# A hybrid encoder layer with PEER experts: U's products in three rounded passes, the dense stage unrolled, and half a tile's expert rows fetched during routing

## The chip, the cores and the metric

One core of a Trainium2 chip runs one launch of the program. The metric is the device time of the launch in microseconds (us); lower is better. Everything is float32 in and out.

## The reference

Attention, projections and norms come first; the part that the change touches is the PEER layer. For each of 1152 tokens (1024 prompt, 128 sample) it takes the 16 best of 128 x 128 experts for each of 8 heads, so 128 experts a token:

```python
def blk(tb):                                   # tb: 128 tokens x 1024
    q = (tb @ wq).reshape(128, 8, 2, 128)
    sc = einsum('thpd,pnd->thpn', q, subkeys)
    sv, si = top_k(sc, 16)
    cand = sv[:, :, 0, :, None] + sv[:, :, 1, None, :]
    cv, ci = top_k(cand.reshape(128, 8, 256), 16)
    e = i1 * 128 + i2                          # i1, i2: si at ci // 16, ci % 16
    g = softmax(cv)
    h = einsum('thkd,td->thk', u[e], tb)
    return einsum('thk,thkd->td', gelu(h) * g, v[e])
```

u and v are 16384 x 1024 each. The result is added to the residual, and a last RMS norm follows.

## The kernel before

The program runs stages one after the other: lead, sample attention, projection (with the fetched rows of the sample tile), window attention, `decide` and `dense`. The change touches the last two.

**decide** (the routing stage) goes over the eight prompt tiles of 128 tokens, i = 1 to 8. In iteration i, TensorE does the stick-breaking attention of tile i (i pairs of blocks, `attend`), then the output projections, the queries of tile i-1 (`queries`, 16 slices w), their scores, and the merge with `w_o`. VectorE meanwhile ranks the scores of tile i-2: `halves_best`, `pairs_best`, `experts_of`, `weigh`; between them it forms the residual (`residual`) and norm of its neighbours. It has about the same order as TensorE, with semaphores in both directions.

A tile is then treated in one of three ways. A *dense* tile (i = 1 to 4) is computed against all experts in `dense`; for it a matrix G of gates (expert x token) must be in memory. For the *sent* tiles (1 to 3) GpSimd scatters the weights into G, one indirect DMA for each of 128 columns, 384 in all (`scatter_head`, L1512). For the *hot* tile (4) TensorE builds G out of one-hot matrices that VectorE makes (`one_hots`), in 32 chunks of four tokens; `WOVEN` says how many chunks go into each attention pair. A *fetched* tile (5 to 8) stores its normed activations, indices and weights.

**dense** has 128 blocks of 128 experts. In block b TensorE does `hidden(b)`, eight float32 products of U's block with the 512 dense tokens, and `values`, eight products for a group of GB = 4 earlier blocks, into four banks. ScalarE applies gelu, VectorE multiplies with G (`gate`) and adds the value banks to qacc (`take`). Beside it run the fetched tiles, 4 rows a block and 512 in all: GpSimd gathers row r of u and v for 128 tokens (`gathers`, 1 MB) into a ring of SL = 8 slots, VectorE multiplies and sums (`products`, two rows), ScalarE takes their gelu, and VectorE adds the weighted v row to acc one pair later (`add_rows`), which frees the slot. The code is in loops whose body covers eight blocks, with waits against registers; the very first body stands outside.

SP issues the loads in one fixed order (L2020 U, L2023 V, L2013 on). U's block b goes into one of GB = 4 buffers and waits for the product of b-4. V has two groups of buffers; the first V load of group n (`v_rows`, j = 0) waits until the values of group n-2 are done, and all later loads stand behind that wait:

```python
sp.dma_start(gb[u][:], o["G"][bass.ts(n, GB)].rearrange("b p t -> p b t")).then_inc(g_in[u], 16)
for j in range(GB):
    u_rows(GB * n + j, j)
    if j == 0 and not (number(n) and n < 2):
        sp.wait_ge(v_done, 2 * DENSE * (n - 1))
        sp.sem_inc(sp_past, 1)
    v_rows(GB * n + j, u, j)
```

## Time and profile before

| | us |
|---|---|
| median of 3 runs | 4029.32 (4026.34 to 4032.59) |
| profiled execution | 4026.89 |
| its span | 4025.2 |
| mean granted clock of TensorE | 0.935 of full speed |

| share of the span | PE | VectorE | ScalarE | GpSimd |
|---|---|---|---|---|
| busy | 88% | 65% | 21% | 41% |

Each engine's busy time comes from its own instructions; loads of TensorE's weights overlap its products. The granted clock is the share of 2.4 GHz that TensorE was given. A float32 product of 512 columns appears as two records, so eight products are 16 records (x16). `decide` runs from about 1100 to 2148 us, `dense` from there to the end. The rows further down are all from this one execution.

### The profile page before, as it was taken

How to read it: one execution, taken by the hardware profiler on the slowest of the kernel's cores; microseconds unless marked ns; L12 is line 12 of the kernel's file. 1: busy time of each engine (PE TensorE's matmuls, PEld its weight loads, DVE VectorE, ACT ScalarE, POOL GpSimd, SP SyncE). 2: the span in 40 equal slices, each digit the busy share in tenths (PEclk: the TensorE clock that was granted, in tenths of full speed). 3: DMA queues.
4: the chain of work that ended last, by engine and by line, in shares of the span. 5: the costliest groups of instructions: out<-in, count | busy, mean ns of one | idle time of the engine just before them, and what ended most of it. 6: DMA issues, size and time to landing. Idle time of an engine off the chain costs nothing. (4 is left out here: it accounts for less than half of the span.)

```text
span 4025.2 us, 44686 instructions
## 1 busy us (share of the span) xinstructions
PE 3549.7 (88%) x14147; PEld 2107.2 (52%) x14147; DVE 2617.7 (65%) x5036; ACT 841.0 (21%) x1599; POOL 1631.8 (41%) x1245
## 2 busy tenths in 40 slices
PE   8997878776699999988862899999999999999998
PEld 6445567776457667656651344444444444444443
DVE  0451878883405435344464988888888878888886
ACT  1451211112423444354510000010001000010001
POOL 0000077770000777777773433334333334333331
PEclk9899889887799999999986999999999999999999
DMA  7793399995765656666856999999999999999994
GB/s 256 315 408 146 105 383 407 384 391 210 254 222 185 151 128 160 143 138 116 169 123 250 391 406 388 388 400 405 400 416 403 397 372 400 388 398 388 382 387 186
DMA packets 424246, 1201.21 MB, mean 298 GB/s; under 512 B 150473, under 2 KB 215417, under 8 KB 345337
## 3 DMA queue, kind: packets, MB, share of 16 engines
q0 software_dynamic: 168496, 680.80, 45.8%
q1 hardware_dynamic: 187600, 505.84, 34.2%
q10 hardware_dynamic: 67968, 12.45, 1.9%
q8 instruction: 78, 1.28, 0.1%
q14 instruction: 104, 0.84, 0.1%
HBM read 1127.33 MB, written 72.68 MB: 298 GB/s over the span
## 5 line engine op out<-in xcount | busy, mean ns | idle before, releaser
L2066 POOL DMA_INDIRECT d_ring<-peer_uv,d_idx x512 | 655.4, 1280 | 1087.6 <-DVEq L2120 981.9
L2223 PE MATMUL d_ps<-d_xd,d_u 128*128 128x512 f32 x2048 | 908.5, 597 | 99.9 <-DMA d_u<-u_blocks 81.1
L2234 PE MATMUL d_ps<-d_v,d_a 128*128 128x512 f32 x2048 | 914.1, 600 | 43.3 <-DVE d_a L2126 36.5
L1512 POOL DMA_INDIRECT G<-c_cellg,c_cell x384 | 617.5, 1608 | 436.6 <-DVE c_cellg L1641 233.5
L2118 DVE SCALAR_TENSOR_TENSOR d_acc<-d_ring,d_aw,d_acc 128x1024 f32<-128x1024 f32 x512 | 657.7, 1285 | 102.1 <-DVE d_acc L2118 66.9
L2223 PEld LDWEIGHTS d_ps<-d_xd,d_u 128*128 128x128 f32 x2048 | 391.8, 192 | 596.0 <-issue 584.3
L2234 PEld LDWEIGHTS d_ps<-d_v,d_a 128*128 128x128 f32 x2048 | 393.3, 193 | 545.5 <-issue 544.8
L2106 DVE SCALAR_TENSOR_TENSOR d_ring<-d_ring,d_xn 128x1024 f32<-128x1024 f32 x512 | 605.9, 1221 | 97.3 <-DMA d_qacc<-ys 51.5
L840 POOL DMA_INDIRECT a_x<-peer_uv,a_rowu x128 | 154.2, 1205 | 547.8 <-DVE a_rowv L910 505.3
L2188 ACT ACTIVATE d_ge<-d_h (+1 forms) x256 | 52.0, 203 | 1204.9 <-DVE d_ring L2106 1204.6
L1037 PE MATMUL a_ps<-a_w_low,a_x_high 128*128 128x256 f32 (+1 forms) x704 | 204.3, 290 | 61.7 <-DVE a_w_low L852 45.8
L1917 PEld LDWEIGHTS c_ps<-c_mT,c_chunk 128*128 128x128 f32 x2048 | 232.3, 194 | 4.9 <-issue 3.4
L1917 PE MATMUL c_ps<-c_mT,c_chunk 128*128 128x128 f32 x2048 | 232.6, 277 | 1.1 <-ACT c_mT L1754 1.1
L1037 PE MATMUL a_ps<-a_w_high,a_x_low 128*128 128x256 f32 (+1 forms) x704 | 202.8, 288 | 0.0
L1037 PE MATMUL a_ps<-a_w_high,a_x_high 128*128 128x256 f32 (+1 forms) x704 | 202.6, 288 | 0.0
L2133 DVE TENSOR_TENSOR d_qacc<-d_ps,d_qacc 128x512 f32<-128x512 f32 x256 | 167.8, 684 | 42.6 <-PE d_ps L2234 42.5
L937 DVE SCALAR_TENSOR_TENSOR k_acc<-a_x,a_gw,k_acc 128x1024 f32<-128x1024 f32 x128 | 164.5, 1285 | 33.4 <-DVE k_acc L937 25.2
L840 POOL DMA_INDIRECT a_x<-peer_uv,a_rowv x128 | 165.5, 1293 | 43.5 <-issue 36.6
L932 DVE SCALAR_TENSOR_TENSOR a_x<-a_x,k_xg 128x1024 f32<-128x1024 f32 x128 | 153.8, 1225 | 35.0 <-DMA a_x<-peer_uv,a_rowu 32.4
L1037 PEld LDWEIGHTS a_ps<-a_w_low,a_x_high 128*128 128x128 f32 x704 | 139.6, 198 | 63.5 <-DVE a_w_low L852 47.4
L1828 PE MATMUL c_ps<-c_q,c_k 64*128 64x128 f32 (+1 forms) x1152 | 158.4, 289 | 14.3 <-DVE c_mask_b L1533 14.2
L1828 PEld LDWEIGHTS c_ps<-c_q,c_k 64*128 64x128 f32 (+1 forms) x1152 | 142.4, 198 | 49.1 <-issue 30.2
(360 smaller groups left out, 4134.4 us busy)
## 6 DMA issues: line engine op xcount, KB each, us to landing
c_chunk<-wq SPq DMA_DIRECT2D x128, 512.0 KB, 5.0
d_u<-u_blocks SPq DMA_DIRECT2D x128, 512.0 KB, 18.7
d_v<-v_blocks SPq DMA_DIRECT2D x128, 512.0 KB, 16.5
s_kc<-sb_kT SPq DMA_DIRECT2D x32, 1024.0 KB, 9.5
s_vc<-sb_v SPq DMA_DIRECT2D x32, 1024.0 KB, 7.4
c_chunk<-w_m SPq DMA_DIRECT2D x64, 512.0 KB, 5.5
d_gb<-G SPq DMA_DIRECT2D x32, 1024.0 KB, 34.5
G<-b_zeros SPq DMA_DIRECT2D x32, 768.0 KB, 8.3
```

The source lines that it names most:

```text
L840: pool.indirect_dma_start(out=ring[:, k % RB], out_offset=None, in_=rows, in_offset=bass.IndirectOffsetOnAxis(ap=source[:, k % P:k % P + 1 ...
L937: nc.vector.scalar_tensor_tensor(acc[:], ring[:, r], aw[:, s:s + 1], acc[:], ALU.mult, ALU.add).then_inc(summed, 1)
L1037: last = nc.tensor.matmul(out, lhsT(left, k), rhs(right, k), start=(k == 0 and n == 0), stop=(k == KC - 1 and n == 2))
L1512: pool.indirect_dma_start(out=grid, out_offset=bass.IndirectOffsetOnAxis(ap=cell[q][:, s:s + 1], axis=0), in_=cell_g[q][:, s:s + 1], in_of ...
L1828: last = nc.tensor.matmul(ps[:, bank + par, c * P:(c + 1) * P], k_sb[p % 2][0:rows, x], q_sb[0:rows, x], start=(c == 0 or n > 0 and stop), ...
L1917: last = nc.tensor.matmul(ps[:, QUERY[w // 4], (w % 4) * P:(w % 4 + 1) * P], wq[:, c * P:(c + 1) * P], xT[:, c], start=(c == 0), stop=(c = ...
L2066: pool.indirect_dma_start(out=ring[:, b], out_offset=None, in_=a["peer_uv"], in_offset=bass.IndirectOffsetOnAxis(ap=idx8[par][:, b:b + 1], ...
L2106: last = nc.vector.scalar_tensor_tensor(ring[:, b, 0:D], ring[:, b, 0:D], 1.0, xn[T % 2][:], ALU.mult, ALU.mult, accum_out=h[:, bass.ds(co ...
L2118: nc.vector.scalar_tensor_tensor(acc[T % 2][:], ring[:, b, D:], aw[:, bass.ds(col + n, 1)], acc[T % 2][:], ALU.mult, ALU.add).then_inc(sum ...
L2133: nc.vector.tensor_tensor(part, ps[:, VB + c % 4, :], part, ALU.add).then_inc(v_taken, 1)
L2223: last = nc.tensor.matmul(ps[:, HB + x % 2, :], ub[j][:, k], xd[:, k].rearrange("p t q -> p (t q)"), start=(k == 0), stop=(k == KC - 1))
L2234: last = nc.tensor.matmul(ps[:, VB + c % 4, :], A[u][j][:, q * P:(q + 1) * P], vb[u][j][:, half * 512:half * 512 + 512], start=(j == 0), s ...
```

## The change

In **dense**, U's block and the dense activations are each split in a high part, which is the value rounded to the narrower format of TensorE's fast float32 mode (`F32R`), and a low part, the rest. `hidden` then does three products, low x high, high x low and high x high, in place of one: 24 a block. ScalarE copies the high part of U (`high`), VectorE subtracts to get the low part (`low`), one block ahead. U's buffers go from four to two, which `low` frees, the ring of rows from eight slots to six. All loops are unrolled and wait on constants; the index copies on GpSimd go. The order of SP's first loads changes; qacc is loaded last.

The **tiles** are shifted: tile 1 is now fetched, tiles 2 to 5 are dense, of which 2 and 3 are sent (256 scatters) and 4 and 5 are hot (64 chunks). Of tile 1's 128 rows, EARLY = 64 are handled in decide: GpSimd gathers the 64 u rows and then the 64 v rows there (4 KB for each token) into a ring of eight, and VectorE takes them at places given by `FETCH`, `LOOKUPS` and `AFTER`. `dense` has 448 rows left, 3.5 a block. Of the 64 chunks, 22 are woven into attention, and 14 each go beside the queries of tiles 6, 7 and 8 (`AMONG`), in banks 6 and 7.

The core of the diff (lines left out where there is "..."):

```diff
-DENSE, HOT = 4, 1
+DENSE, HOT = 4, 2
 FIRST_HOT = DENSE - HOT
 FETCHED = NT - 1 - DENSE
+EARLY = 64
...
-    WOVEN = [[0] * i for i in range(NT - 2)] + [[0] + [2] * 6, [0] + [3] * 6 + [2]]
+    WOVEN = [[0] * i for i in range(NT - 2)] + [[0, 2, 2, 2, 2, 1, 1], [0, 2, 2, 2, 2, 2, 1, 1]]
+    AMONG = 14
+    RB = 8
+    FETCH = [[0] * i for i in range(4)] + [[3, 3, 4, 4], [3, 3, 4, 4, 4], [2, 3, 3, 3, 3, 2], [2] * 7, [1] * 8]
+    LOOKUPS = [0, 0, 0, 0, 6, 6, 6, 0, 0]
+    AFTER = [0, 0, 0, 14, 6, 0, 2, 6, 4]
+    GELU_AT = 5
...
-    dense = lambda i: 1 <= i <= DENSE
-    hot_tile = lambda i: FIRST_HOT < i <= DENSE
-    sent = lambda i: 1 <= i <= FIRST_HOT
-    fetched = lambda i: i > DENSE
+    dense = lambda i: 2 <= i <= DENSE + 1
+    hot_tile = lambda i: 2 + FIRST_HOT <= i <= DENSE + 1
+    sent = lambda i: 2 <= i < 2 + FIRST_HOT
+    fetched = lambda i: i == 1 or i > DENSE + 1
+    rank = lambda i: 0 if i == 1 else i - DENSE - 1
+    among = lambda j: AMONG if j >= NT - 3 else 0
...
+                def gather(n):
+                    for k in range(issued[0], min(issued[0] + n, 2 * EARLY)):
+                        at = k % EARLY
+                        source = row_u if k < EARLY else row_v
+                        if k >= RB:
+                            pool.wait_ge(freed, k - RB + 1)
+                        pool.indirect_dma_start(out=ring[:, k % RB], out_offset=None, in_=rows,
+                                                in_offset=bass.IndirectOffsetOnAxis(ap=source[:, at:at + 1], axis=0)).then_inc(filled[k % RB], 16)
+                    issued[0] += n
...
+                pool.wait_ge(rows_ready, 3)
+                gather(RB + AFTER[3] + sum(FETCH[4]) + LOOKUPS[4] + AFTER[4])
+                for n in range(44):
+                    scatter(2)
+                    gather(1)
+                while sends[0] < P * FIRST_HOT:
+                    scatter(min(5, P * FIRST_HOT - sends[0]))
+                    gather(1)
+                gather(2 * EARLY - issued[0])
+                pool.wait_ge(scattered, 16 * P * FIRST_HOT)
...
                     for n, (table, test) in enumerate(((rise, ALU.is_ge), (pos[:, :, 1, 1:17], ALU.is_equal))):
+                        beside(3 * n)
                         step(nc.vector.tensor_tensor(hot, place[:, n, :, :, None].to_broadcast([P, 8, 16, 16]),
                                                      digit[:, n, None, None, :].to_broadcast([P, 8, 16, 16]), test), f"hot{n + 1}", j)
+                        beside(3 * n + 1)
...
+                def fetch(n):
+                    for k in range(fetches[0], fetches[0] + n):
+                        r, s = k % RB, k % EARLY
+                        if k == EARLY:
+                            dve.wait_ge(act_e, 1)
+                            nc.vector.tensor_tensor(aw[:, 0:EARLY], h_sb[:, 0:EARLY], gw_first[:, 0:EARLY], ALU.mult).then_inc(dve_e, 1)
+                            dve.wait_ge(dve_e, 1)
+                        dve.wait_ge(filled[r], 16 * (k // RB + 1))
+                        if k < EARLY:
+                            nc.vector.scalar_tensor_tensor(ring[:, r], ring[:, r], 1.0, xg[:], ALU.mult, ALU.mult,
+                                                           accum_out=h_sb[:, s:s + 1]).then_inc(freed, 1)
+                        else:
+                            if s:
+                                dve.wait_ge(summed, s)
+                            nc.vector.scalar_tensor_tensor(acc[:], ring[:, r], aw[:, s:s + 1], acc[:], ALU.mult, ALU.add).then_inc(summed, 1)
+                            dve.wait_ge(summed, s + 1)
+                            dve.sem_inc(freed, 1)
+                    fetches[0] += n
...
                         one_hots(WOVEN[i][n])
+                        fetch(FETCH[i][n])
...
-                    experts_of(i - 2)
+                    mixed = among(i - 1)
+                    one_hots(min(2, mixed))
+                    experts_of(i - 2, lambda n: (one_hots(mixed * (n + 1) // 7 - mixed * n // 7), fetch(LOOKUPS[i] // 6)))
+                    one_hots(mixed - min(2, mixed) - mixed * 6 // 7)
                     weigh(i - 2)
+                    fetch(AFTER[i])
...
-                halves_best(NT - 2)
+                halves_best(NT - 2, lambda n: one_hots((3, 3, 3, 3, 2)[n]))
+                fetch(2 * EARLY - fetches[0])
...
+                        for w in range(4 * g, 4 * g + 4):
+                            take(1 if w >= 16 - among(j) else 0, BESIDE)
...
+                    if i == GELU_AT:
+                        act.wait_ge(freed, EARLY)
+                        nc.scalar.activation(h_sb[:, 0:EARLY], h_sb[:, 0:EARLY], ACT.Gelu).then_inc(act_e, 1)
...
+                        if w == 16 - among(j) and j < NT - 1:
+                            pe.wait_ge(dve_m.sem, dve_m.at(j + 1, "gated_b"))
+                        spread_out(1 if w >= 16 - among(j) else 0, BESIDE)
...
-    SL = 8
-    TB = P // FETCHED
+    SL = 6
+    NU, NS = 2, 2
...
+    TILES = [0] + list(range(DENSE + 1, NT - 1))
+    STARTS = [0] + [P - EARLY + P * k for k in range(FETCHED)]
+    ROWS = STARTS[-1]
+    PAIRS = ROWS // 2
+    pairs_in = lambda b: range(PAIRS * b // P, PAIRS * (b + 1) // P)
...
+                def u_rows(b):
+                    if b >= NU:
+                        sp.wait_ge(u_split, b - NU + 1)
+                    sp.dma_start(ub[b % NU][:], a["u_blocks"][b]).then_inc(u_in[b % NU], 16)
+                def v_rows(b):
+                    n, u, j = b // GB, b // GB % 2, b % GB
+                    if n >= 2 and j == 0:
+                        sp.wait_ge(v_done, VC * (n - 1))
                     sp.dma_start(vb[u][j][:], a["v_blocks"][b]).then_inc(v_in[u], 16)
...
+                for n in range(2):
+                    sp.dma_start(xd[:, 4 * n:4 * n + 4], o["xd"][:, 4 * n:4 * n + 4].rearrange("p k t q -> p k (t q)")).then_inc(xd_in[n], 16)
+                    u_rows(n)
+                gates(0)
+                v_rows(0)
                 for dst, src in ((gw[:], o["gw"].rearrange("t p s -> p t s")), (gf[:], bass.AP(a["gf"].tensor, 0, [[0, P], [1, D]]))):
                     sp.dma_start(dst, src).then_inc(tabs, 16)
...
-                sp.dma_start(qacc[:], o["ys"][0:DENSE].rearrange("t p d -> p t d")).then_inc(qacc_in, 16)
...
+                for j in range(1, GB):
+                    if j > 1:
+                        u_rows(j)
+                    v_rows(j)
+                sp.dma_start(qacc[:], o["ys"][1:1 + DENSE].rearrange("t p d -> p t d")).then_inc(qacc_in, 16)
+                for n in range(1, NG):
+                    for j in range(GB):
+                        u_rows(GB * n + j)
+                        if j == 0:
+                            gates(n)
+                        v_rows(GB * n + j)
...
+                def low(b):
+                    dve.wait_ge(u_high_done, b + 1)
+                    nc.vector.tensor_tensor(u_low[b % NS][:], ub[b % NU][:], u_high[b % NS][:].bitcast(F32), ALU.subtract).then_inc(u_split, 1)
...
+                for b in range(P):
+                    if b:
+                        gate(b - 1)
+                    if b + 1 < P:
+                        low(b + 1)
+                    for c in (2 * (b - 1) % VC, 2 * (b - 1) % VC + 1):
+                        n = b // GB - 1 - (b % GB == 0)
+                        if n == 0 and c == 0:
+                            dve.wait_ge(qacc_in, 16)
+                        if n >= 0:
+                            take(n, c)
+                    for p in pairs_in(b):
+                        products(p)
+                        if p:
+                            add_rows(p - 1)
...
+                def high(b):
+                    act.wait_ge(u_in[b % NU], 16 * (b // NU + 1))
+                    if b >= NS:
+                        act.wait_ge(h_done, b - NS + 1)
+                    nc.scalar.activation(u_high[b % NS][:], ub[b % NU][:], ACT.Copy).then_inc(u_high_done, 1)
...
-                def hidden(b, x, j, round):
-                    pe.wait_ge(u_in[j], 16 * (round + 1))
-                    if not (number(b) and b < 2):
+                def hidden(b):
+                    pe.wait_ge(u_split, b + 1)
+                    if b >= 2:
                         pe.wait_ge(h_gelu, b - 1)
+                    x_parts, u_parts = (x_high, x_low), (u_high[b % NS], u_low[b % NS])
                     for k in range(KC):
-                        last = nc.tensor.matmul(ps[:, HB + x % 2, :], ub[j][:, k], xd[:, k].rearrange("p t q -> p (t q)"), start=(k == 0), stop=(k == KC - 1))
+                        if b == 0:
+                            pe.wait_ge(x_split, k + 1)
+                        for n, (left, right) in enumerate(((0, 1), (1, 0), (0, 0))):
+                            last = nc.tensor.matmul(ps[:, HB + b % 2, :], u_parts[left][:, k], x_parts[right][:, k],
+                                                    start=(k == 0 and n == 0), stop=(k == KC - 1 and n == 2))
                     last.then_inc(h_done, 1)
```

## Rows read from the trace of the kernel before

**Rows 1.** Windows: stretch, length; PE, PEld, DVE, ACT, POOL busy; clock, DMA share, GB/s

```profile
1174.00:2148.00 974.00, 836.60 (x5027) 620.18 (x5024) 463.98 (x1948) 373.22 (x565) 617.52 (x384) 0.93 0.63 145
...
2240.00:3985.00 1745.00, 1710.01 (x3952) 754.07 (x3952) 1481.65 (x2119) 147.60 (x400) 658.68 (x562) 0.99 0.98 390
...
2590.00:3100.00 510.00, 510.00 (x1189) 225.63 (x1188) 442.14 (x634) 48.46 (x124) 197.60 (x169) 1.00 1.00 405
...
2784.00:2788.00 4.00, 4.00 (x10) 1.71 (x9) 3.48 (x5) 0.20 (x1) 1.29 (x2) 1.00 1.02 424
```

**Rows 2.** The chain that ended last, in order of time: start us, us, what

```profile
2733.76 6.87 PE d_ps L2234 x16
2740.62 6.87 PE d_ps L2223 x16
```

**Rows 3.** Timeline of PE in projection, first and last of 48 records: start, us, what

```profile
589.69 0.39 PE L1037 MATMUL a_ps<-a_x_low,a_w_high 128*128 128x512 f32 x1
...
600.65 0.40 PE L1037 MATMUL a_ps<-a_x_high,a_w_high 128*128 128x512 f32 x1
```

**Rows 4.** Timeline of VectorE, one looped block: its gate, its first product, the next gate

```profile
2712.37 0.69 DVE L2126 TENSOR_TENSOR d_a<-d_a,d_gb 128x512 f32<-128x512 f32 x1 [0.23 <-DVE d_acc L2118]
...
2714.18 1.22 DVE L2106 SCALAR_TENSOR_TENSOR d_ring<-d_ring,d_xn 128x1024 f32<-128x1024 f32 x1
...
2725.49 0.69 DVE L2126 TENSOR_TENSOR d_a<-d_a,d_gb 128x512 f32<-128x512 f32 x1 [0.23 <-DVE d_acc L2118]
```

**Rows 5.** The chain in the unrolled first body: starts of two neighbouring pairs of rows

```profile
2207.78 2.37 DVE d_ring L2106 x4
...
2213.14 0.21 DVE d_ring L2106
```

**Rows 6.** Groups of 1024 columns: the residual on VectorE, a copy on ScalarE

```profile
L1556 DVE TENSOR_TENSOR c_y<-c_ps,c_y x7: 1224/1225/1227, 1236.9 to 2044.4; 128x1024 f32<-128x1024 f32 x7
...
L1754 ACT ACTIVATE c_mT<-c_ps 128x1024 f32<-128x1024 f32 x8 | 8.2, 1023 | 5.8 <-PE c_ps L1909 5.8
```

**Rows 7.** A group's second U load: issue and landing; landing of one at 2687

```profile
2741.45 0.33 SPq L2020 DMA_DIRECT2D d_u<-u_blocks  x1
...
DMA to landing us min/median/max: 10.9/10.9/10.9
...
DMA to landing us min/median/max: 8.5/8.5/8.5
```

**Rows 8.** Landing of the gathers issued in 2744 to 2748, and in 2784 to 2788

```profile
DMA to landing us min/median/max: 13.8/13.8/13.8
...
DMA to landing us min/median/max: 6.8/6.9/7.1
```

**Rows 9.** VectorE: last weights of decide (duration ns, first and last start), first product of dense

```profile
L1641 DVE TENSOR_TENSOR c_g<-c_g,c_gsum x5: 291/292/293, 1668.8 to 2145.4; 128x128 f32<-128x128 f32 x5
...
2199.45 1.22 DVE L2106 SCALAR_TENSOR_TENSOR d_ring<-d_ring,d_xn 128x1024 f32<-128x1024 f32 x1 [51.54 <-DMA d_qacc<-ys]
```

**Rows 10.** GpSimd: the scatters of decide, and gathers of 4 KB rows in projection

```profile
L1512 POOL DMA_INDIRECT G<-c_cellg,c_cell x384: 1534/1542/3116, 1317.5 to 2136.5; - x192
...
L840 POOL DMA_INDIRECT a_x<-peer_uv,a_rowv x128 | 165.5, 1293 | 43.5 <-issue 36.6 <-DVEq L939 6.9
```

**Rows 11.** Timeline of VectorE: two one-hot chunks in succession

```profile
1703.68 0.69 DVE L1654 TENSOR_TENSOR c_first<-c_iota,c_turned 128x512 f32<-128x512 f32 x1
...
1705.30 0.69 DVE L1654 TENSOR_TENSOR c_first<-c_iota,c_turned 128x512 f32<-128x512 f32 x1
```

**Rows 12.** Timeline of PE: ends of attention in iterations 6 to 8, and 16 query slices

```profile
1623.74 0.39 PE L1938 MATMUL c_ps<-c_mask_b,c_zero_b 128*128 128x512 bf16 x1
...
1790.37 0.39 PE L1938 MATMUL c_ps<-c_mask_b,c_zero_b 128*128 128x512 bf16 x1
...
1805.28 28.75 PE L1917 MATMUL c_ps<-c_mT,c_chunk 128*128 128x128 f32 x256
...
1981.75 0.39 PE L1938 MATMUL c_ps<-c_mask_b,c_zero_b 128*128 128x512 bf16 x1
```

413 lines of the change are left out of this document (192 added, 221 removed).

## The prediction, made before the change was run

> **What bounds the kernel now.** I read the windows first. The dense stage, from about 2148 us to the end, holds 1877 of the 4025.2 us. In it TensorE is busy without a gap for 510 us, at the full granted clock (1.00, the 2.4 GHz level), while the DMA engines move 405 GB/s at a busy share of 1.00 and VectorE works 442 of the 510 us [rows 1]. The chain shows why: eight products of U, then eight of V, 6.87 us each, back to back, so a block of 128 experts takes 13.74 us [rows 2]. Over the whole stage PE idled only 35 of 1745 us. Routing (1174 to 2148 us) is PE's too, 837 of 974 us, with VectorE busy 464, GpSimd 618 (its scatters), and DMA at 145 GB/s [rows 1]. So the stages have one master, but in the dense stage two others stand right behind it, VectorE at 87% and DMA near its ceiling. The most that I see DMA move in any stretch is 424 GB/s [rows 1].
>
> **The dense stage, engine by engine.**
> U on PE: 24 products over rounded parts replace 8 full ones. The projection stage runs the same form, 128x512 out of rounded parts, with starts 0.233 us apart (10.96 us for 47 steps) [rows 3]; 24 x 0.233 = 5.60 us against 6.87. PE's block becomes 5.60 + 6.87 = 12.47 us, 163 us less over 128 blocks.
> VectorE: now a block starts every 13.12 us, of which 1.81 go to the gate and two takes and 11.31 to four rows [rows 4]. Where that code is unrolled (block 0, whose body is outside the loops) a pair of rows takes 2213.14 - 2207.78 = 5.36 us [rows 5], against 5.66 looped. The change unrolls all of it and leaves 1.75 pairs in a block: 9.38 us. It adds low(b), a subtraction of 128x1024, as long as the residual's 1.225 us [rows 6], 1.15 net of the overlap of neighbours. Block: 1.81 + 9.38 + 1.15 = 12.34 us. Nothing is won on VectorE by this beyond 0.8 us: rows leave, the splitting comes.
> ScalarE: high(b), a copy of 1024 columns, 1.02 us [rows 6], on an engine that is idle for most of the stage; it costs only as a link in the chain below.
> DMA: 448 rows x 1.05 MB, U and V 67 MB each, G 34 MB = 638 MB; at 420 GB/s 1519 us, 11.9 us a block.
> So by engines alone a block would be 12.47 us. Three things are within 5% of each other, hence what decides is how they wait for one another.
>
> The wait that I expect: u_rows(4n+1) stands in SP's queue behind v_rows(4n), which waits until PE has finished block 4n-1; call that moment t. Today the second U load of a group is issued 0.8 us after t (2741.45 against a block start at 2740.62) and lands 10.9 or 8.5 us later [rows 2, 7]. PE needs it 13.74 us after t, and nobody else does. After the change VectorE must split it one block ahead: low(4n+1), near the start of block 4n, waits for the load, then for high (1.0 us). Queued behind low on VectorE are both takes, all row work and the next gates; with two U buffers for four SP's u_rows(4n+3), and the loads behind it, wait for that low too. With landing time L, VectorE is through low at t + 0.8 + L + 1.0 + 1.2 = t + 3.0 + L. It then has 4 x 12.34 - 1.9 = 47.5 us of work to the gate that PE's values(4n+4) wait for, 0.7 more with that gate; PE follows with 6.87 + 3 x 12.47 = 44.3 us. Two groups therefore take 3.0 + L + 47.5 + 0.7 + 44.3 = 95.5 + L, so a group of four takes 51.8 (L 8.5) to 53.2 us (L 10.9). When VectorE stands still, no ring slot is freed and gathers pause, so L should fall; at L 6 it is 50.8. I take 51.5, 12.87 us a block, and carry the present 35 idle us over 127 blocks (0.28) along: **13.15 us a block**. Ends: 12.5 (no wait) and 13.9.
>
> The ring of 8 becomes 6. A row's slot cycle is then 6 x 13.15 / 3.5 = 22.5 us; a row is held about 11.4 us between its product and its sum (two pair steps and part of the block's other work), which leaves 11 for issue and landing. Gathers land in 13.8 us just after the V and U loads were issued and in 6.9 when those are through [rows 8]. On average that fits, in the burst not; this is the upper end.
>
> Edges: VectorE's first product now starts at 2199.45, 51 us into the stage, behind a load of all qacc [rows 9]. The new order puts qacc late and has about 5.3 MB ahead of the norm weights against 7.5, so some 32 us; PE's split of the activations (8 copies, 8 subtractions, 10 us) hides under it. The first four blocks have no takes (-7). The last 35 us (V's last group, sums of squares, stores) stay. Stage: 32 + 128 x 13.15 - 7 + 35 = 1743 us, against 1877: **-134**.
>
> **Routing.** Scatters fall from 384 to 256, at 820 / 384 = 2.14 us of GpSimd each [rows 10]; 128 gathers come at 1.3 + 0.3 us [rows 10], and the hot chunks rise from 32 to 64.
> Rows 0 to 63 cost VectorE 1.36 us each for a product and 1.42 for a sum, 178 us in all, in a stage where it stands idle 510 of 974 us [rows 1]. I cost them at 5 us: the 14 after tile 1's weights start before their data can be there (GpSimd starts at 1317.5 [rows 10]), so the next residual is about 16 us late and its square on ScalarE 5. If that cover were gone they would cost up to 178.
> Chunks: VectorE makes one in 1.62 us [rows 11]. PE's own part is half of a query slice: 28.75 / 16 / 2 = 0.9 us [rows 12]. Woven into attention a chunk costs more: stage 8 is 191.4 us with 20, stage 7 166.6 with 12 [rows 12]; the 24.8 us between them are eight chunks and one more pair, so a chunk is between 0.9 and 3.1; I take 2. Stage 7 loses 2 chunks (-4), stage 8 loses 8 (-16). Fourteen among the queries: PE needs 14 x 2.7 + 3.6 = 41 us, VectorE as long (14 x 1.62 and experts_of), against 28.75: +13, with the last wait +16, in both. At the tail VectorE has 14 chunks (22.7) and eight sums (11.4), +34, on the chain from the last residual (2044.4 [rows 6]) to the last weights (2145.4 [rows 9]), which it works through without rest.
> GpSimd: scatters can start only when it has issued 48 gathers and tile 2's weights exist. Those of tile 1 come at 1317, and the stages, 166.6 us long at the seventh, are shorter here; with 115 us for one and VectorE's lateness (an estimate) that is 1450 us. Then 44 rounds of 2 scatters and 1 gather (5.9 us) reach 92 gathers at about 1707, and rounds of 5 and 1 (12.3 us) end near 2125. Stage 7 wants gathers 89 to 102 in a stretch where 5:1 gives half of that; I put +28 there. Sum: 5 - 4 + 16 + 28 - 16 + 16 + 34 = +79. If stage 7 is not held, the tail waits for the last gather at about 2137 instead, +66. I take **+72**; ends +40 and +110.
>
> Sum: 4025.2 - 134 + 72 = 3963, and 1.7 us around the span give **3965 us**, 1.5% less. The profiled execution was 4026.9 us, the median of the runs 4029.3, so the difference is not worth correcting.
>
> **Two rules of the Trainium skill.** The trace shows 405 GB/s held for 510 us [rows 1]. "DMA: Bandwidth & Descriptors", section Bandwidth, says that for transfers between HBM and SBUF the HBM side binds, at about 358 GB/s. By that the 638 MB would need 1781 us and this change would gain nothing. The trace disagrees, and the sum goes by the trace.
> A gather's landing doubles from 6.9 to 13.8 us beside the bulk loads [rows 8]. The same page, section Queues, rings and completion order, has each DMA engine take turns between the queues it has work for, packet by packet. By that rule the gathers get no priority however few there are, which speaks for the third rival; the trace agrees so far, and its price is worked out there from rows.
>
> **Rivals.**
> Close to the engines' bound: the paused gathers let U land at once, a block is 12.6 us, 70 us less: 3895. For it: DMA's average need falls to 12 us a block. Against: VectorE 12.34 and PE 12.47 leave no slack for each other's waits. Chance 0.25.
> The forecast, 3930 to 4010 by its terms: 0.45.
> Slower: the two-deep U buffers and the six-slot ring. Two waits for gathers of 2 to 3 us in each group's burst, on top of L = 10.9, give 53.2 + 3 = 56.2 us a group, with the idle part 14.0 a block: 3965 + 128 x 0.85 = 4070, about 4050 with routing at its low side. It decides from 13.63 us a block on, where 128 x 0.48 eats the 62 us. Chance 0.20. At 13.55 to 13.7 it is no change: 0.07.
> The passes do not get cheaper (24 products at more than 0.286 us, since here the weights change source each time): 4110; 0.03, the projection stage alternates in the same way.
>
> **Chances.** Faster by over 0.2% (what a measurement here can tell from none): 0.25 + 0.45 = 0.70; within: 0.07; slower: 0.23. The range 3880 to 4058 leaves out the worst of routing with the third rival, and the passes.
>
> **What would show it.** Right: U's matmuls 0.233 us apart; a PE wait or a VectorE wait behind d_u or d_uh once every four blocks, of 5 us or more on VectorE; stage from 2220 to 3963; ACT's copy of U at 1.0 us; GpSimd's last scatter near 2125; waits for c_ring in stage 7. Wrong: waits for d_ring above 3 us a group (the ring), a routing stage that ends within 30 us of 2148 (gathers not in the way), or beyond 2260.

## The result, and the profile after

The changed kernel takes **4157.2 us** (median; 4152.8 to 4164.9) beside 4030.9 for the kernel before: ratio **1.032, 95% interval 1.030 to 1.034**. It is slower by 126 us where the prediction had it faster by 64. Its profiled execution has a span of 4151.1 us.

Two stages matter. Their borders are two loads in SP's timeline, that of the identity for routing and that of the dense activations (`xd`) for the dense stage:

| stage, us | before | after | forecast change | measured change |
|---|---|---|---|---|
| all ahead of routing | 1087.1 | 1075.8 | 0 | -11 |
| routing | 1061.0 | 1217.9 | +72 | **+157** |
| dense | 1877.1 | 1857.4 | -134 | **-20** |

What lies ahead of routing is the same code; over all runs here it took 1074 to 1092 us, so stages are compared by their own length. With the changed kernel's code in it, routing took 1211 to 1232 us. The runs were made in groups, each on one chip: up to 20 us lie between groups, about 4 within one. The changed kernel's dense stage took 1857 to 1873 us in the four executions whose edits leave it alone; differences under some 15 us say nothing there.

Windows of the changed kernel, columns as in [rows 1]: a steady part of the dense stage, routing, and two stretches of one group of four blocks.

```profile
2600.00:3100.00 500.00, 455.62 (x1425) 272.41 (x1426) 422.78 (x578) 68.37 (x137) 205.12 (x128) 0.95 0.92 357
1174.00:2294.00 1120.00, 875.75 (x5249) 658.84 (x5247) 670.12 (x2304) 404.70 (x597) 582.86 (x384) 0.89 0.74 192
2823.00:2845.00 22.00, 21.81 (x74) 13.60 (x73) 15.26 (x22) 3.02 (x5) 7.60 (x5) 1.00 0.98 383
2845.00:2873.00 28.00, 27.70 (x88) 16.11 (x86) 25.03 (x36) 3.69 (x8) 12.46 (x8) 1.00 0.88 329
```

No engine is full any more. PE is busy 91% (before: all of it), VectorE 85%, the DMA engines move 357 GB/s instead of 405. With no engine full, what is lost must be waits of one for another. Who waits stands in the groups of VectorE over the whole kernel (instructions, busy us, mean ns | idle us before them and what ended it):

```profile
L2182 DVE SCALAR_TENSOR_TENSOR d_ring<-d_ring,d_xn 128x1024 f32<-128x1024 f32 x448 | 536.6, 1221 | 132.1 <-DMA d_ring<-peer_uv,d_idx 117.2 <-DVE d_acc L2198 14.6
L2173 DVE TENSOR_TENSOR d_ul<-d_u,d_uh 128x1024 fp32r<-128x1024 f32 x128 | 155.9, 1218 | 69.0 <-ACT d_uh L2264 50.5 <-DMA d_gf<-gf 18.5
```

117 us for rows that have not landed, 50 for the rounded copy of U. The two next views are timelines: SP's issues in one group of the dense stage, as in [rows 7], and on PE the ends of attention in iterations 6 to 8, as in [rows 12].

```profile
2822.99 0.33 SPq L2106 DMA_DIRECT2D d_v<-v_blocks  x1
2823.36 0.43 SPq L2100 DMA_DIRECT2D d_u<-u_blocks  x1
...
2825.16 0.50 SPq L2106 DMA_DIRECT2D d_v<-v_blocks  x1
2835.24 0.33 SPq L2100 DMA_DIRECT2D d_u<-u_blocks  x1
...
2844.18 0.43 SPq L2111 DMA_DIRECT2D d_gb<-G  x1
2872.73 0.33 SPq L2106 DMA_DIRECT2D d_v<-v_blocks  x1
```

```profile
1632.05 0.39 PE L2024 MATMUL c_ps<-c_mask_b,c_zero_b 128*128 128x512 bf16 x1
...
1805.64 0.39 PE L2024 MATMUL c_ps<-c_mask_b,c_zero_b 128*128 128x512 bf16 x1
...
2031.58 0.39 PE L2024 MATMUL c_ps<-c_mask_b,c_zero_b 128*128 128x512 bf16 x1
```

SP sends five loads in 2.7 us, four more by 2844, then none for 28 us: V's wait for PE stands at the head of the queue. In routing, the stretch from the end of one attention to the end of the next takes 173.6 us for iteration 7 (before 166.6) and 225.9 for iteration 8 (191.4).

Routing's waits in the changed kernel, from the list of waits of 1290 to 2293 us (who, for whom: us in total, times, longest):

```profile
ACT c_spread L1784 <- DMA G<-c_spread: 97.6, 5, 25.3
DVE c_acc L1707 <- DMA c_ring<-peer_uv,c_rowv: 75.1, 14, 13.3
PE c_ps L1898 <- ACT c_spread L1784: 54.0, 3, 21.5
PE c_ps L1898 <- DVE c_second L1725: 24.2, 2, 17.8
DVE c_ring L1702 <- DMA c_ring<-peer_uv,c_rowu: 16.3, 6, 5.6
```

The first line is the store of eight finished chunks to G (2 MB in pieces of 128 B, issued by ScalarE): one buffer, so ScalarE cannot take the ninth chunk until it has landed, 13.5 to 26.2 us later, and behind ScalarE stands PE (third line). The kernel before had this wait too, without PE behind it:

```profile
ACT c_spread L1710 <- DMA G<-c_spread: 39.2, 3, 14.3
```

### The profile page after: what moved, and what is told of

Read it like the earlier page. It is cut to its first block and busy times, and to the rows that moved or that the text cites. A ratio compares the mean times of both kernels' runs of the same rounds, so it can differ in the third digit from the quotient of the medians.

```text
span 4151.1 us, 43335 instructions
## 1 busy us (share of the span) xinstructions
PE 3450.0 (83%) x15430; PEld 2346.3 (57%) x15430; DVE 2829.8 (68%) x5304; ACT 976.3 (24%) x1729; POOL 1649.4 (40%) x1121
## 5 line engine op out<-in xcount | busy, mean ns | idle before, releaser
L2155 POOL DMA_INDIRECT d_ring<-peer_uv,d_idx x448 | 731.6, 1633 | 1045.6 <-DVEq L2200 957.0
L2198 DVE SCALAR_TENSOR_TENSOR d_acc<-d_ring,d_gw,d_acc 128x1024 f32<-128x1024 f32 x448 | 575.4, 1284 | 44.6 <-DVE d_acc L2198 36.4
L2314 PE MATMUL d_ps<-d_x_low,d_uh 128*128 128x512 f32 x1024 | 451.1, 441 | 131.5 <-DVE d_ul L2173 131.4
L1541 POOL DMA_INDIRECT G<-c_cellg,c_cell x256 | 430.2, 1680 | 126.5 <-issue 73.5
L2314 PE MATMUL d_ps<-d_x_high,d_ul 128*128 128x512 f32 x1024 | 402.6, 393 | 0.0
L2314 PE MATMUL d_ps<-d_x_high,d_uh 128*128 128x512 f32 x1024 | 402.3, 393 | 0.0
L2314 PEld LDWEIGHTS d_ps<-d_x_low,d_uh 128*128 128x128 f32 x1024 | 194.8, 190 | 202.8 <-DVE d_ul L2173 138.8
L2314 PEld LDWEIGHTS d_ps<-d_x_high,d_ul 128*128 128x128 f32 x1024 | 194.9, 190 | 64.3 <-issue 27.7
L2314 PEld LDWEIGHTS d_ps<-d_x_high,d_uh 128*128 128x128 f32 x1024 | 194.2, 190 | 41.6
L1528 POOL DMA_INDIRECT c_ring<-peer_uv,c_rowu x64 | 82.0, 1281 | 313.4 <-DVE c_rowv L1678 225.6
L2173 DVE TENSOR_TENSOR d_ul<-d_u,d_uh 128x1024 fp32r<-128x1024 f32 x128 | 155.9, 1218 | 69.0 <-ACT d_uh L2264 50.5
```

What stands on the lines that cost most here:

```text
L1528: pool.indirect_dma_start(out=ring[:, k % RB], out_offset=None, in_=rows, in_offset=bass.IndirectOffsetOnAxis(ap=source[:, at:at + 1], axi ...
L1541: pool.indirect_dma_start(out=grid, out_offset=bass.IndirectOffsetOnAxis(ap=cell[q][:, s:s + 1], axis=0), in_=cell_g[q][:, s:s + 1], in_of ...
L2155: pool.indirect_dma_start(out=ring[:, r % SL], out_offset=None, in_=a["peer_uv"], in_offset=bass.IndirectOffsetOnAxis(ap=idx[:, k % 2, s:s ...
L2173: nc.vector.tensor_tensor(u_low[b % NS][:], ub[b % NU][:], u_high[b % NS][:].bitcast(F32), ALU.subtract).then_inc(u_split, 1)
L2198: nc.vector.scalar_tensor_tensor(acc[k % 2][:], ring[:, r % SL, D:], gw[:, k, s + n:s + n + 1], acc[k % 2][:], ALU.mult, ALU.add).then_inc ...
L2314: last = nc.tensor.matmul(ps[:, HB + b % 2, :], u_parts[left][:, k], x_parts[right][:, k], start=(k == 0 and n == 0), stop=(k == KC - 1 an ...
```

## Experiments in the dense stage

Each is an edit of the changed kernel. The tables give the kernel's time, its ratio to the kernel before on the same chip, and the length of the stage in question.

**One load moved**

```diff
-                        u_rows(GB * n + j)
+                        if j != 1:
+                            u_rows(GB * n + j)
                         if j == 0:
                             gates(n)
+                            u_rows(GB * n + 1)
                         v_rows(GB * n + j)
```

> The changed kernel with one load moved: in SP's queue the second U load of a group now stands ahead of the first V load, whose wait for PE it stood behind. Theory A, VectorE's own work (12.6 us a block in the trace of after) plus its waits set the dense stage: the 50 us that the subtraction waits for the rounded copy of U go, the waits for gathers stay near 117 us, and the kernel takes 40 to 50 us less. Theory B, the DMA engines (busy share 0.92) have no more to give: the U load takes the gathers' time, VectorE's waits for ring slots grow by what the others lose, and the time stays within 10 us.

**Eight slots**

```diff
-    SL = 6
+    SL = 8
...
-        x_high, x_low = sb("d_x_high", [P, KC, Q], F32R), sb("d_x_low", [P, KC, Q], F32R)
+        x_high = x_low = sb("d_x_high", [P, KC, Q], F32R)
...
```

> The changed kernel with eight ring slots in the dense stage instead of six. The room comes from the low parts of the activations, which are not made: those products read the high parts, so their values differ while the number and form of the matmuls stay. Theory A: VectorE's waits for gathers fall from 117 us to under 30, and the dense stage of 1857 us loses 80 to 110 us (the waits for the rounded copy of U may grow by 10). Theory B, the DMA engines are the bound: waits move to the U loads, and the stage loses under 20 us.

**Five slots** (SL = 5, nothing else)

> The changed kernel with five ring slots instead of six. Theory A: a gather has one slot less, a sixth of the slot cycle of 24 us or 4 us less for issue and landing, on each of 448 rows; where it was late already (a third of the rows) that shows in full: the stage grows by 150 to 400 us. Theory B: transfers are merely spread differently, under 40 us more.

**No subtraction**

```diff
-                    nc.vector.tensor_tensor(u_low[b % NS][:], ub[b % NU][:], u_high[b % NS][:].bitcast(F32), ALU.subtract).then_inc(u_split, 1)
+                    dve.sem_inc(u_split, 1)
...
-                    x_parts, u_parts = (x_high, x_low), (u_high[b % NS], u_low[b % NS])
+                    x_parts, u_parts = (x_high, x_low), (u_high[b % NS], u_high[b % NS])
```

> The changed kernel without VectorE's subtraction for the low part of U: PE's 24 products read the high part in its place, so their values differ and PE's work stays. VectorE's block falls from 12.6 to 11.5 us. Theory A, VectorE's work and waits add up: 1.14 us x 128 = 146 us less, down to PE's own 12.33 us a block, so 130 to 150 us less for the stage of 1857. Theory B, the transfers set the pace: VectorE's waits for gathers grow from 117 to over 200 us and the stage loses under 50.

| run | time, us | ratio (95%) | dense stage | against 1857 to 1873 |
|---|---|---|---|---|
| one load moved | 4156.8 | 1.029 (1.027 to 1.030) | 1847 | -10 to -26 |
| eight slots | 4121.5 | 1.020 (1.018 to 1.022) | 1805 | -52 to -68 |
| five slots | 4653.1 | 1.153 (1.150 to 1.156) | 2342 | +469 to +485 |
| no subtraction | 4146.9 | 1.027 (1.025 to 1.029) | 1841 | -16 to -32 |

Theory A (VectorE's work and waits add up) missed three of its four numbers, and exceeded the fourth. Yet B, that the DMA engines can give no more, cannot explain 470 us for one slot. What A lacked shows in the same groups of VectorE, with one load moved, with eight slots, and with five (there only the first of the two):

```profile
L2184 DVE SCALAR_TENSOR_TENSOR d_ring<-d_ring,d_xn 128x1024 f32<-128x1024 f32 x448 | 538.2, 1222 | 163.4 <-DMA d_ring<-peer_uv,d_idx 148.8 <-DVE d_acc L2200 14.0
L2175 DVE TENSOR_TENSOR d_ul<-d_u,d_uh 128x1024 fp32r<-128x1024 f32 x128 | 156.0, 1219 | 25.0 <-DMA d_gf<-gf 18.9 <-ACT d_uh L2266 6.1
```

```profile
L2182 DVE SCALAR_TENSOR_TENSOR d_ring<-d_ring,d_xn 128x1024 f32<-128x1024 f32 x448 | 530.3, 1221 | 24.0 <-DVE d_acc L2198 14.9 <-DMA d_ring<-peer_uv,d_idx 8.9
L2173 DVE TENSOR_TENSOR d_ul<-d_u,d_uh 128x1024 fp32r<-128x1024 f32 x128 | 156.1, 1220 | 141.9 <-ACT d_uh L2264 118.4 <-DMA d_gf<-gf 23.5
```

```profile
L2182 DVE SCALAR_TENSOR_TENSOR d_ring<-d_ring,d_xn 128x1024 f32<-128x1024 f32 x448 | 547.6, 1223 | 655.6 <-DMA d_ring<-peer_uv,d_idx 646.6 <-DVE d_acc L2198 9.1
```

The wait aimed at did go each time (50 to 6, 117 to 9), and the other one grew (117 to 149, 50 to 118). While VectorE stands still for one transfer, the other one lands. VectorE's time is still its work plus its waits (the account below), but a wait can't be taken off it as if the others stayed. The run without the subtraction says the same: 146 us of work less, 103 us of waits more (181 for rows, 90 for U).

So the next question was whether both waits together are worth more than the sum. The lead time of a row can be read in the trace. GpSimd's two gathers after a stop (first view: changed kernel, timeline of GpSimd; second: VectorE):

```profile
2840.61 1.93 POOL L2155 DMA_INDIRECT d_ring<-peer_uv,d_idx  x1 [10.98 <-DVEq L2200]
2842.84 1.74 POOL L2155 DMA_INDIRECT d_ring<-peer_uv,d_idx  x1 [0.30 <-issue]
```

```profile
2839.00 1.28 DVE L2198 SCALAR_TENSOR_TENSOR d_acc<-d_ring,d_gw,d_acc 128x1024 f32<-128x1024 f32 x1
...
2850.45 1.23 DVE L2182 SCALAR_TENSOR_TENSOR d_ring<-d_ring,d_xn 128x1024 f32<-128x1024 f32 x1 [0.15 <-DVE d_acc L2198]
...
2853.02 1.22 DVE L2182 SCALAR_TENSOR_TENSOR d_ring<-d_ring,d_xn 128x1024 f32<-128x1024 f32 x1 [1.34 <-DMA d_ring<-peer_uv,d_idx]
```

The sum that starts at 2839.00 frees a slot; the gather into it starts at 2840.61, its pair's second at 2842.84, and VectorE wants that second row at 2851.7, 8.8 us later, with a gate, a subtraction and two takes in between. Gathers land after 6.4 to 11.4 us in this stretch, after 5.2 to 17.0 (median 8.8) in the whole stage. Without those four operations the lead is 3.1 us shorter. Four of six slots are held by two pairs in work; only two can be under way. Taken row by row, as in runs below, no row waits for a partner, and a gather has four row steps of 2.6 us and the block's other work before its row is wanted: in the run with even loads one issued at 2808.39 is wanted at 2821.75, 13.4 us later.

**Loads spread evenly over the blocks**

```diff
-                for n in range(1, NG):
-                    for j in range(GB):
-                        u_rows(GB * n + j)
-                        if j == 0:
-                            gates(n)
-                        v_rows(GB * n + j)
+                for m in (4, 5, 6):
+                    u_rows(m)
+                gates(1)
+                for b in range(GB, P):
+                    if b + 3 < P:
+                        u_rows(b + 3)
+                    v_rows(b)
+                    if b % GB == 2 and b // GB + 1 < NG:
+                        gates(b // GB + 1)
```

> The changed kernel with SP's loads of the dense stage in another order: in each block one U load three blocks ahead, then one V load, and G two blocks after the V wait, so that V's wait for PE has no load behind it that could have gone. In the changed kernel's trace SP issues five loads in 2.7 us (2823 to 2826 us), four more by 2844, then none until 2873, while the DMA engines go between 420 and 285 GB/s. Theory C, VectorE starves in the burst and the DMA engines in the gap: evenly spread, the gathers' landing stays under 9 us, VectorE's waits for gathers fall from 117 to under 50 us and those for the copy of U from 50 to under 10, so 60 to 110 us less. Theory D, the engines cannot move more than some 360 GB/s in this mix of transfers: within 15 us.

**Row by row, gate's multiplication on ScalarE** (and the even loads)

```diff
-                        products(p)
-                        if p:
-                            add_rows(p - 1)
+                        for r in (2 * p, 2 * p + 1):
+                            product(r)
+                            if r:
+                                add_row(r - 1)
...
-                    nc.vector.tensor_tensor(gw[:, k, s:s + 2], h[:, s:s + 2], gw[:, k, s:s + 2], ALU.mult).then_inc(weighed, 1)
+                    nc.scalar.activation(h[:, s:s + 1], h[:, s:s + 1], ACT.Copy, scale=gw[:, k, s:s + 1]).then_inc(row_gelu, 1)
```

> The paced order of loads as in the run before, and the rows taken one by one: product r, then the sum of row r-1, with the gate's multiplication moved from VectorE to ScalarE. Two to four ring slots are held instead of up to five, and VectorE loses 0.33 us a block. Theory C, the ring's slots decide: against the paced order alone the waits for gathers fall by another 30 us or more and the stage by 40 to 80 us. Theory D: no difference beyond 15 us. A third way: ScalarE's two small operations (0.4 us and their hand-overs) do not fit under one product of 1.14 us, and VectorE waits 0.3 us on each of 448 rows, so that 50 to 130 us are lost.

**Eight slots and even loads** (both edits above together)

> The changed kernel with eight ring slots and the paced order of loads together (room as in the run with eight slots: the low parts of the activations are not made, products read the high parts). Alone, the slots gave 36 us and the order nothing. Theory G, lead time: with pairs and six slots the gather for a pair's second row is issued one pair step and one product (5.4 + 1.1 = 6.5 us, 9.6 where a gate and takes lie between) ahead of its use, and lands after 6.4 to 11.4 us; eight slots add 5.4 us. A late row and a late U load hide each other, so that taking away one shows the other. Both away: 150 to 200 us less than the changed kernel, as in the row by row run. Theory H, the row by row run won by the operation it took from VectorE: here under 60 us less.

**Row by row with the old order of loads**

> The changed kernel with rows taken one by one and the gate's multiplication on ScalarE, but with the changed kernel's own order of loads. Theory G: a gather's lead is four row steps, 10.8 us or more, so the ring waits go; the U load behind V's wait stays (50 us in the changed kernel, some 90 when the rows do not hide it), so 80 to 150 us of the 206 remain. If the order of loads adds nothing at all: all of the 206. If it was the order that let the rows win: under 40.

**Row by row, even loads, multiplication on VectorE**

> The row by row kernel with the paced order of loads, but with the gate's multiplication kept on VectorE, one element a row: 448 operations of 0.19 us with their gap, 0.66 us a block instead of none. Theory G: lead time is what counts; the kernel loses 128 x 0.66 = 84 us at most against the row by row run if VectorE is the bound there, and still stands 110 us or more under the changed kernel. Theory H, the operation taken from VectorE is what won: it is no better than the changed kernel (within 20 us).

| run | time, us | ratio (95%) | dense stage | VectorE waits for rows / U | sum of VectorE |
|---|---|---|---|---|---|
| after | 4157.2 | 1.032 (1.030 to 1.034) | 1857 | 117 / 50 | 1849 |
| one load moved | | | 1847 | 149 / 6 | 1837 |
| even loads | 4164.8 | 1.034 (1.031 to 1.037) | 1871 | 177 / 1 | 1860 |
| eight slots | | | 1805 | 9 / 118 | 1809 |
| eight slots, even loads | 4021.6 | 0.996 (0.994 to 0.998) | 1721 | 14 / 12 | 1708 |
| row by row, old loads | 4083.7 | 1.009 (1.006 to 1.012) | 1772 | 21 / 111 | 1771 |
| row by row, even loads | **3958.5** | **0.983 (0.980 to 0.986)** | **1672** | 21 / 1 | 1662 |
| the same, mult. on VectorE | 4055.3 | 1.002 (1.001 to 1.004) | 1742 | 13 / 1 | 1738 |
| no subtraction | | | 1841 | 181 / 90 | 1808 |

The table's last column is VectorE's account: 128 blocks at 12.6 us (below) plus 34 us of start, 35 of end, and the two waits; row by row takes 42 us off (the pair's multiplication, 0.19 us x 1.75 x 128), the variant on VectorE adds 42 instead, no subtraction takes 146 off. It comes within 13 us in all but the last, where it is 33 short (there VectorE also waits 41 us for PE's V products).

Even loads alone give nothing (1871 is in the changed kernel's own range, so D's number came out, though not for D's reason), eight slots alone 52; together 137. Lead time decides, and it pays only when the U load is on time too; theory G's 150 for them was missed narrowly. Row by row alone gives 85, with even loads 185 (its seven executions lie between 1668 and 1673). Moving the multiplication to ScalarE is worth 1742 - 1672 = 70 us of that, below the bound of 84 that was expected; with the multiplication back on VectorE the kernel is still 116 us under the changed kernel in this stage, so H (the operation alone) falls. Theory D falls with the windows of the row by row run, which moves what the kernel before moved:

```profile
2600.00:3100.00 500.00, 490.12 (x1579) 297.62 (x1578) 458.23 (x578) 129.56 (x361) 230.51 (x143) 0.99 0.99 397
```

## Experiments in routing

**The store in wide pieces**

```diff
-                            act.dma_start(o["G"][:, :, col:col + TS].rearrange("b p t -> p b t"), spread[:]).then_inc(G_st, 16)
+                            act.dma_start(o["G"][16 * u:16 * u + 16, :, FIRST_HOT * P:].rearrange("b p t -> p b t"),
+                                          spread[:].rearrange("p e t -> p (e t)").rearrange("p (b t) -> p b t", t=HOT * P)).then_inc(G_st, 16)
```

> The changed kernel with the store of the spread weights in pieces of 1 KB instead of 128 B: the same bytes go into the same region of G, in another order, so the values are not the reference's. Theory E, ScalarE cannot take the next chunk until this store has landed (five waits of 19 to 25 us, 98 in all), and PE stands behind it (54 us in three waits): the store takes under 8 us and routing gets 35 to 55 us shorter. Theory F, the chunks' own work on VectorE and PE fills these waits anyway: under 10 us.

**No early rows** (the loops of gathers, products and sums run over nothing)

> The changed kernel without the 64 early rows in routing: no gathers, products or sums of theirs, so half of tile 1's row sum is missing from the output. It prices them: the prediction had 5 us of lateness, 28 in stage 7 and 11 at the tail, 44 in all. If they cost that, routing ends 40 to 50 us earlier (2245 to 2255 instead of 2293); if VectorE's waits for gathers (75 us) and the lateness that they hand to PE count in full, 70 to 100 us earlier; if the store of the chunks is what ends last in stages 7 and 8 anyway, under 25.

**Both**

> The changed kernel with both edits in routing: no early rows, and the chunks' store in pieces of 1 KB (half of one tile's row sum missing, G's hot part in another order). If the two causes are independent, routing takes 1218 - 38 - 59 = 1121 us, 60 above the kernel before, and those 60 are chunks and queries. If one hides the other, 1140 or more. If both together were the whole excess (each covering a part of the other's cost), 1061 to 1095.

**Another pace of GpSimd**

```diff
-                for n in range(44):
-                    scatter(2)
-                    gather(1)
+                while issued[0] < 2 * EARLY:
+                    scatter(1)
+                    gather(1)
...
```

> The row by row kernel with another order of GpSimd's work in routing: after the first 48 gathers one scatter to each gather until the gathers are out, then the rest of the scatters, in place of two and then five scatters to a gather. VectorE's waits for gathers of V rows in stages 7 and 8 (66 us in the changed kernel) go, since the last gather is issued some 100 us earlier; the last scatter ends near 2112 us as before, 170 us ahead of routing's end. If those waits reach PE in full, routing ends 30 to 55 us earlier; if ScalarE's wait for the store of the chunks takes their place, under 15.

**Chunks placed otherwise**

```diff
-    WOVEN = [[0] * i for i in range(NT - 2)] + [[0, 2, 2, 2, 2, 1, 1], [0, 2, 2, 2, 2, 2, 1, 1]]
-    AMONG = 14
+    WOVEN = [[0] * i for i in range(NT - 2)] + [[0] + [3] * 6, [0] + [3] * 7]
+    AMONG = {NT - 3: 8, NT - 2: 9, NT - 1: 8}
...
```

> The row by row kernel with paced loads, with the 64 chunks placed otherwise in routing: 18 and 21 woven into the attention of stages 7 and 8 in place of 10 and 12, and 8, 9 and 8 among the queries in place of 14 each, so that no store of eight chunks has to land between two chunks of one series of queries. Theory E (PE's 54 us behind three stores): 17 chunks more in attention at 2 us each cost 34, 17 fewer beside the queries give back some 20, and the 54 us go: routing 25 to 45 us shorter than the 1211 us of the row by row run. Theory F (the chunks' work is what costs, wherever it lies): within 12 us.

**Rows used later** (FETCH of stages 7 and 8 from 2 and 1 to 1 and 2 a piece; three scatters between gathers instead of five)

> The row by row kernel with paced loads, with the early rows used later: in stage 7 one row in each piece of attention instead of two, in stage 8 two instead of one, and three scatters instead of five between two gathers once 92 are out. VectorE's waits for V rows in stages 7 and 8 (66 us) fall under 20. If they reach PE, through the one-hots that stand behind them, routing is 15 to 35 us shorter than 1211; if PE waits for the chunks' store anyway, under 8.

**Both of these**

> Row by row, paced loads, later rows and the chunks placed otherwise, all values as in the reference. If the two routing edits add up, routing is 40 to 75 us shorter than 1211 and the kernel takes 3885 to 3920 us where the kernel before takes some 4030; if the later rows crowd VectorE in stage 8, where 21 chunks now lie, 10 to 30 us of it are lost.

**Two buffers for the store**

```diff
-    RB = 8
+    RB = 4
...
-        spread = sb("c_spread", [P, P, TS])
+        spreads = [sb(f"c_spread{n}", [P, P, TS]) for n in range(2)]
...
```

> The row by row kernel with two buffers for the chunks' store instead of one, and four slots in routing's ring of rows instead of eight, which is what makes the room. Theory E: ScalarE's waits for the store (98 us) fall under 10 and routing gets 30 to 50 us shorter than 1211 us, unless the gathers take it back: with four slots VectorE's waits for rows may grow from 80 us to 150, and where they do by that much routing is no shorter than 1211.

**Two buffers, rows later**

> The same with the rows used later (one in each piece of stage 7, two in stage 8) and three scatters between two gathers once 92 are out. With the store out of the way the waits for rows can reach PE, so what gave 7 us alone gives 15 to 30 here: routing 1140 to 1175 us, and the kernel some 3890 to 3930 us beside 4030 of the kernel before. If it gives under 8 again, VectorE's waits for rows in stages 7 and 8 are covered by something else.

| run | dense part as in | time, us | ratio (95%) | routing |
|---|---|---|---|---|
| wide store | after | 4122.7 | 1.023 (1.020 to 1.026) | 1179 |
| no early rows | after | 4108.7 | 1.020 (1.016 to 1.023) | 1158 |
| both | after | 4064.8 | 1.008 (1.005 to 1.010) | 1115 |
| other pace | row by row | 4169.8 | 1.032 (1.029 to 1.035) | 1406 |
| chunks elsewhere | row by row | 3961.3 | 0.982 (0.980 to 0.984) | 1206 |
| later rows | row by row | 3965.0 | 0.982 (0.979 to 0.984) | 1204 |
| both of these | row by row | 3964.6 | 0.982 (0.980 to 0.985) | 1210 |
| two buffers | row by row | 3945.3 | 0.979 (0.977 to 0.980) | 1200 |
| two buffers, later rows | row by row | **3922.3** | **0.973 (0.970 to 0.976)** | **1173** |

Routing without an edit took 1211 us in the group of the wide store and the run without rows, so these two give 32 and 53 us, 85 in sum. The later groups had no run with routing unedited, so they are compared by their ratios: both edits together stand 2.4% below the changed kernel (1.008 against 1.032), 97 us. They add up, neither covers the other. Over the kernel before, 54 us of routing remain (1115 against 1061). In that run ScalarE still waits 62.0 us for the store, and PE 26.7 us behind it; the rest would be the chunks' own part and the queries beside them, which no run took apart.

The wide pieces were to land in under 8 us. The trace has no landing for them, but where ScalarE waited, its next chunk starts as the store lands. The same store in the changed kernel and with wide pieces (timelines of ScalarE):

```profile
1852.25 0.38 ACTq L1789 DMA_DIRECT2D G<-c_spread  x1
...
1878.53 1.89 ACT L1784 ACTIVATE c_spread<-c_ps 128x512 f32<-128x512 f32 x2 [25.26 <-DMA G<-c_spread]
```

```profile
1851.84 0.38 ACTq L1789 DMA_DIRECT2D G<-c_spread  x1
...
1868.57 1.88 ACT L1784 ACTIVATE c_spread<-c_ps 128x512 f32<-128x512 f32 x2 [15.71 <-DMA G<-c_spread]
```

Read like this, five stores took 13.8 to 26.3 us in the changed kernel (mean 20.8) and five 7.3 to 16.7 with wide pieces (12.9). Without early rows it was 13.7 to 23.0 (18.8) and, wide, 7.0 to 14.4 (12.2). So the wider pieces (their size and their place in G changed together) made the store 7 to 8 us shorter, not as short as expected, and ScalarE's wait fell from 98 to 58 us. With two buffers the wait is gone from the list. In its place stand the waits for rows, 261 us instead of 91, because the ring gave up four slots for it (waits of the run with two buffers):

```profile
DVE c_acc L1707 <- DMA c_ring<-peer_uv,c_rowv: 205.1, 37, 13.8
...
DVE c_ring L1702 <- DMA c_ring<-peer_uv,c_rowu: 55.9, 28, 7.7
```

By its ratio the kernel gains 0.45% over the row by row run (0.983), some 18 us; the two intervals (0.977 to 0.980 and 0.980 to 0.986) just touch. Rows used later bring the first of these waits down again, and the gain becomes 1.0%, some 40 us, clear of both intervals (two buffers, later rows):

```profile
DVE c_acc L1707 <- DMA c_ring<-peer_uv,c_rowv: 122.5, 28, 9.5
```

The same later rows gave nothing that can be measured with one buffer (0.982 beside 0.983, as with the chunks elsewhere, and with both), although VectorE's wait for V rows from 1640 us on fell from 66 to 24 us in that run. That it was covered is the likely reading; no run isolates it. Moving chunks from the queries into attention gave nothing either. ScalarE's wait for the store only moved along (97.0 us in six waits). PE stands behind the chunks 15.4 us instead of 54.0, but 38.2 us behind other work of ScalarE, the copy of the queries (23.9) and the softmax (14.3), for which it had no such wait before the move. It is ScalarE that stands; theory E had counted only the chunks that stand behind it.

The other pace cost some 176 us (1406 against the 1228 to 1232 of its group): GpSimd issues in order, and a gather that waits for a free slot holds the scatters behind it. Its wait for a slot that a sum must free is 367 us where the changed kernel has 20, and its last scatter starts at 2484.9 instead of 2127.6:

```profile
POOL c_ring L1528 <- DVEq L1706: 367.5, 23, 131.2
```

The last row of the table computes what the reference computes and beats both kernels, by 2.7% and by 5.7% (3922.3 against 4157.2, without an interval of their own).

## Why the prediction was wrong, step by step

**PE.** Forecast 5.60 and 6.87 us; measured in the chain 5.45 and 6.87. Right, a little better than said.

```profile
3016.07 6.87 PE d_ps L2327 x16
3022.94 5.45 PE d_ps L2314 x24
3028.39 6.87 PE d_ps L2327 x16
```

**VectorE.** Forecast 12.34 us a block. Three blocks with two pairs take 13.9 us each and one with a single pair 8.6, 12.6 on average: 0.26 too low, some 33 us over the stage. The pairs are 5.36 to 5.38 us apart as in [rows 5]; gate, subtraction and takes need 3.14 where 2.96 were summed.

**ScalarE.** The copy 1.02 us, measured 1.05. Right.

**U behind V in SP's queue.** The mechanism was right: every fourth block the subtraction waits, 5.5 us at 2833.98. Over the stage that was 50.5 us, and alone worth 10 to 26, because rows landed meanwhile. (One of the sums is off: 95.5 + 8.5 is 104.0 for two groups, so 52.0 for one and not 51.8. The 51.5 that was taken lies below both.)

**The ring: the step that failed.** "A row is held about 11.4 us ..., which leaves 11 for issue and landing ... On average that fits". The average of a slot's cycle says nothing of the pair's second row, whose gather is issued 2.2 us behind the first, and whose lead is 8.8 us with a gate and takes between and less without. I had the landing time of [rows 8], 6.9 to 13.8, and set it against 11. So the forecast put the waits for rows at nothing, and they were 117 us. Of the 114 us by which the stage missed, the waits make 64: the forecast's 13.15 less 12.34 is 104 us over 128 blocks, for U and the idle part together, and 168 were measured (117 for rows, 50 for U). VectorE's work makes 33, start and end 9; 8 are not accounted for.

The forecast had named "waits for d_ring above 3 us a group" as a sign of being wrong. They are 30.2 us in the nine groups from 2600 to 3100 us, 3.4 a group, and 3.7 over the stage. That is the third rival's mechanism, and a chance of 0.20 was too little for it. Its number, 1743 + 109 = 1852 beside 1857, agrees partly by luck. Its 56.2 us a group are 14.05 a block before the idle part of 0.28, which its 14.0 was to hold; with it the stage would be 1894. And the waits were 87 of 1.35 us on average, 2.7 a group, not two of 2 to 3 us.

**DMA.** The 638 MB were no bound: 357 GB/s are what the waits left, and the row by row run moves 397 with the same bytes. The 358 GB/s that "DMA: Bandwidth & Descriptors" of the Trainium skill gives in its section Bandwidth had been set aside in the forecast. The 357 looks like it by chance, and the 397 of the row by row run again disagrees with it. The Trainium skill's "Perfetto Trace Analysis", section Roofline, says that a single core can exceed this share up to some 435 GB/s; with that the traces agree (405 and 397 GB/s held, 424 at most).

**The edge.** First product 32 us into the stage; measured 2327.56 - 2293.70 = 33.9. Right.

```profile
2327.56 1.22 DVE L2182 SCALAR_TENSOR_TENSOR d_ring<-d_ring,d_xn 128x1024 f32<-128x1024 f32 x1
```

**Routing.** By iterations, from the matmuls above and VectorE's last residual and last weights (changes against before):

| part | forecast | measured |
|---|---|---|
| up to the end of attention 6 (less the earlier start) | +5 | +20 |
| to the end of attention 7 | -4 + 28 | +7 |
| to the end of attention 8 | -16 + 16 | +35 |
| to the last residual | +16 | +41 |
| to the last weights | +34 | +53 |

```profile
L1592 DVE TENSOR_TENSOR c_y<-c_ps,c_y x7: 1218/1225/1225, 1226.9 to 2135.6; 128x1024 f32<-128x1024 f32 x7
...
L1687 DVE TENSOR_TENSOR c_g<-c_g,c_gsum x5: 291/291/292, 1682.4 to 2289.9; 128x128 f32<-128x128 f32 x5
```

Stage 7, where I had put the late gathers, is the only part that was better than said. GpSimd's order was forecast well: scatters first at 1438.1 (1450 forecast), last at 2127.6 (2125). What failed is a term that was missing: the chunks were priced on VectorE and PE, and the store that every eight of them set off was not, though its wait of 39.2 us on ScalarE stood in the trace of before. In the last three parts one such store each falls into a series of queries, and PE stands 21.5, 17.4 and 15.2 us behind it. Read from these waits that is 54 of the 79 us by which these parts exceeded the forecast; by experiment, a store 7 to 8 us shorter, with the wide pieces, gave 32 us. And rows cost some 53 us where 44 were said. The stage ended at 2293.7 us, beyond the 2260 that was to show the forecast wrong.

## What to carry over

Count a ring's slack by the worst row: from the instruction that frees the slot to the one that needs the new data, in the consumer's order of work, against the slowest landing seen in the trace; an average cycle hides a pair's second row. Where two kinds of transfers are late on one engine they cover each other, so an edit that removes one wait may show nothing until the other is gone as well; try them together before dropping either. When work is multiplied, follow what each piece sets off (here a store with one buffer), not only the engine that makes it.
